# A transformer block with product-key experts: a shorter candidate list, fewer tiles ahead, and low parts summed by DMA

## The reference

```
q = (ht @ w_query).reshape(N, 8, 2, 128)
s1 = q[:, :, 0] . sub_keys_1 ; s2 = q[:, :, 1] . sub_keys_2      # 128 scores each
t1, i1 = top_k(s1, 16) ; t2, i2 = top_k(s2, 16)
cand = t1[..., :, None] + t2[..., None, :]                       # 256 pairs
sc, pos = top_k(cand.reshape(N, 8, 256), 16)
eidx = i1[pos // 16] * 128 + i2[pos % 16]
gate = softmax(sc)
out = sum over picks of gate * gelu(x . expert_down[eidx]) * expert_up[eidx]
```

## Time and profile before

| | |
|---|---|
| median of 3 runs | 1526.71 us (1525.58 to 1527.91) |
| profiled execution | 1529.9 us, span 1528.0 us |
| PE busy | 1503.2 us (98%) |
| DVE busy | 1226.5 us (80%) |
| ACT busy | 629.1 us (41%) |
| POOL busy | 534.3 us (35%) |
| PE clock granted | 0.997 |
| DMA | 378.94 MB, mean 248 GB/s |

### The profile page before, as it was taken

One profiled execution on the slowest core, in us unless ns is written; L12 is line 12 of the kernel. 1 busy time (PEld: TensorE's weight loads), 2 busy tenths in 40 slices (PEclk: granted clock), 3 DMA queues, 4 the chain that ended last, 5 costly groups with the idle time before them and its releaser, 6 DMA issues.

```text
span 1528.0 us, 22468 instructions
## 1 busy us (share of the span) xinstructions
PE 1503.2 (98%) x8379; PEld 1345.0 (88%) x8379; DVE 1226.5 (80%) x2329; ACT 629.1 (41%) x1050; POOL 534.3 (35%) x357
## 2 busy tenths in 40 slices
PE   9999999999999999999999999999999999999997
PEld 6888888889899999998888888999999999999996
DVE  5577885449999999975776776888888889888885
ACT  6247675332222356663333333333333333333335
POOL 0323102055755710002111112555555556555530
PEclk9999999999999999999999999999999999999999
DMA  8302003323323668889999989999999999999971
GB/s 313 146 25 87 1 2 128 117 89 112 131 60 114 173 208 307 320 307 368 299 309 301 302 293 339 363 367 370 356 361 370 362 371 361 369 367 356 371 254 69
DMA packets 148507, 378.94 MB, mean 248 GB/s; under 512 B 11792, under 2 KB 76688, under 8 KB 145456
## 3 DMA queue, kind: packets, MB, share of 16 engines
q1 hardware_dynamic: 100400, 201.84, 38.3%
q0 software_dynamic: 37200, 138.56, 24.5%
q10 hardware_dynamic: 10800, 37.11, 6.6%
HBM read 338.60 MB, written 38.86 MB: 247 GB/s over the span
## 4 chain that ended last, share of the span: by engine, by line
PE 85%; DVE 10%; DMA 2%; ACT 1%; issue 1%; SPq 0%; DVEq 0%; ACTq 0%
PE bank L1898 22%; PE bank L1803 20%; PE bank L1524 12%; PE bank L1904 11%; PE bank L1812 10%; PE bank L1735 2%; DVE oh L1406 2%; DVE gp L1414 2%; DVE gp L1411 2%; DVE oh L1409 2%; PE bank L1719 1%; DVE d_lo L1395 1%; DMA w_raw<-wts 1%; PE bank L1644 1%; PE bank L1821 1%
## 5 line engine op out<-in xcount | busy, mean ns | idle before, releaser
L1803 PE MATMUL bank<-h_hi,d_hi 128*128 128x384 f32 x1024 | 349.2, 341 | 1.1 <-DVE h_lo L1260 1.1
L1803 PE MATMUL bank<-h_lo,d_hi 128*128 128x384 f32 x1024 | 344.9, 337 | 0.0
L582 POOL DMA_INDIRECT p_in<-rows,p_row x128 | 160.5, 1254 | 403.7 <-DVE p_dot L1433 186.0
L582 POOL DMA_INDIRECT p_in<-up,p_row x128 | 172.0, 1344 | 191.5 <-DVE p_dot L1433 97.1
L1812 PE MATMUL bank<-h_hi,d_lo 128*128 128x384 f32 x1024 | 200.2, 338 | 0.0
L1803 PEld LDWEIGHTS bank<-h_hi,d_hi 128*128 128x128 f32 x1024 | 192.5, 188 | 4.0 <-issue 1.3
L1803 PEld LDWEIGHTS bank<-h_lo,d_hi 128*128 128x128 f32 x1024 | 192.4, 188 | 3.2
L1898 PE MATMUL bank<-u_hi,w_hi_e 128*128 128x512 f32 x750 | 192.2, 392 | 1.3 <-DVE w_lo_e L1458 1.3
L1898 PE MATMUL bank<-u_hi,w_lo_e 128*128 128x512 f32 x750 | 191.0, 390 | 0.0
L1904 PE MATMUL bank<-u_lo,w_hi_e 128*128 128x512 f32 x750 | 190.8, 390 | 0.0
L1812 PEld LDWEIGHTS bank<-h_hi,d_lo 128*128 128x128 f32 x1024 | 180.8, 188 | 0.0
(11 more groups left out here) (290 smaller groups left out, 2438.8 us busy)
## 6 DMA issues: line engine op xcount, KB each, us to landing
d_raw<-down SPq DMA_DIRECT2D x128, 512.0 KB, 5.7
u_raw<-up SPq DMA_DIRECT2D x128, 512.0 KB
gates_dram<-ev ACTq DMA_DIRECT2D x12, 2048.0 KB, 6.7
g_e<-gates_dram SPq DMA_DIRECT2D x32, 768.0 KB
w_raw<-wts SPq DMA_DIRECT2D x9, 2048.0 KB, 8.3
act_dram<-f_act ACTq DMA_DIRECT2D x59, 192.0 KB
a_e<-act_dram SPq DMA_DIRECT2D x59, 192.0 KB
xt<-x_in SPq DMA_DIRECT2D x2, 2048.0 KB, 11.1
```

The lines of the kernel that those rows point to most:

```text
L582: pool.indirect_dma_start(out=p_in[n % GR][:], out_offset=None, in_=rows if kind == "D" else up.rearrange("n p d -> (n p) d"), in_offset=b ...
L1803: nc.tensor.matmul(bank[6 + e % 2][:, 0:TD], d_hi[e % DH_R][:, k], h[:, k, 0:TD], start=(k == j == 0), stop=False)
```

## The change

- **Candidates.** With both lists sorted, pair (i, j) can be among the best 16 only where few pairs dominate it. Rows are cut by runs: row 0 keeps 16 columns, rows 1 and 2 keep 8, rows 3 to 6 keep 4, rows 7 to 14 keep 2, row 15 keeps 1: 65 pairs. They are added by five operations over all four token blocks, and the top 16 is sought among 65. All runs have 16 elements, but for the last, so the column is the position masked by 15 >> (position >> 4). The row is found by comparing the position with the start of each row (is_ge, a staircase in place of a one-hot), and the first key's indices are turned into differences so that the staircase sums to the index.
- **Tiles ahead.** E_SLOTS is 24 instead of 33. E_DVE is 26, E_GATES 28, NE 50. POOL_KEYS is moved to earlier tiles.
- **Low parts.** For tiles 3 to 20 (18 tiles) ACT writes −raw, rounded, to one of three d_sum tiles, and POOL issues a DMA that adds raw to it. POOL no longer subtracts there. PE waits for f_summed0 to 2.
- Several semaphores are merged; cstb_loaded becomes part of cst_loaded.

```diff
-E_SLOTS = 33
+E_SLOTS = 24
+ACC_FROM, ACC_TO = DH_R, E_SLOTS - 3
+def summed(f):
+    return ACC_FROM <= f < ACC_TO
+def sums(f):
+    return 16 * sum(g % 3 == f % 3 for g in range(ACC_FROM, f + 1))
-POOL_KEYS = {6: 0, 8: 1, 11: 2, 13: 3, 16: 4, 20: 5, 25: 6}
+POOL_KEYS = {6: 0, 8: 1, 10: 2, 12: 3, 15: 4, 17: 5, 21: 6}
+RUNS = [(0, 1, 16), (1, 2, 8), (3, 4, 4), (7, 8, 2), (15, 1, 1)]
...
-            sp.dma_start(cstb[:], consts_b[:, 0:6 * P]).then_inc(S("cstb_loaded"), 16)
+            sp.dma_start(cstb[:], consts_b[:, 0:6 * P]).then_inc(S("cst_loaded"), 16)
...
             def early_low(f):
+                if summed(f):
+                    pool.wait_ge(S("d_neg_done"), f - ACC_FROM + 1)
+                    pool.dma_start(d_sum[f % 3][:], d_raw[f % DR][:], accum_op=ALU.add)\
+                        .then_inc(S(f"f_summed{f % 3}"), 16)
+                    return
...
+                if summed(e):
+                    nc.scalar.activation(d_sum[e % 3][:], d_raw[e % DR][:], ACT.Copy, scale=-1.0).then_inc(S("d_neg_done"), 1)
                 nc.scalar.activation(d_hi[e % DH_R][:], d_raw[e % DR][:], ACT.Copy).then_inc(S("d_hi_done"), 1)
...
+            link(V.memset(fifteen[:], TOPK - 1))
...
-                for b in range(TB):
-                    V.tensor_tensor(cand[:, b], tv[r][0][:, b].unsqueeze(2).broadcast_to([P, TOPK, TOPK]),
-                                    tv[r][1][:, b].unsqueeze(1).broadcast_to([P, TOPK, TOPK]), ALU.add)\
-                     .then_inc(S("cand_done"), 1)
+                for q, (first, n, m) in enumerate(RUNS):
+                    at_q = ROW_STARTS[first]
+                    V.tensor_tensor(cand[:, :, at_q:at_q + n * m].rearrange("p b (i j) -> p b i j", j=m),
+                                    tv[r][0][:, :, first:first + n].unsqueeze(3).broadcast_to([P, TB, n, m]),
+                                    tv[r][1][:, :, 0:m].unsqueeze(2).broadcast_to([P, TB, n, m]), ALU.add)\
+                     .then_inc(S("pair_step"), 1)
...
-                V.tensor_copy(tif[r][0][:], ti[r][0][:])
+                V.tensor_scalar(quart[:], posn[:], 4, None, ALU.logical_shift_right).then_inc(S("pair_step"), 1)
+                V.tensor_copy(dif[r][:], ti[r][0][:]).then_inc(S("pair_step"), 1)
                 V.tensor_copy(tif[r][1][:], ti[r][1][:])
-                V.tensor_scalar(pab[r][0][:], posn[:], 4, None, ALU.logical_shift_right)
-                link(V.tensor_scalar(pab[r][1][:], posn[:], TOPK - 1, None, ALU.bitwise_and))
+                dve.wait_ge(S("pair_step"), 9 * hd + 6)
+                V.tensor_tensor(low_bits[:], fifteen[:], quart[:], ALU.logical_shift_right).then_inc(S("pair_step"), 1)
+                dve.wait_ge(S("pair_step"), 9 * hd + 7)
+                V.tensor_copy(tif[r][0][:, :, 0:1], dif[r][:, :, 0:1])
+                V.tensor_tensor(tif[r][0][:, :, 1:TOPK], dif[r][:, :, 1:TOPK], dif[r][:, :, 0:TOPK - 1], ALU.subtract)
+                dve.wait_ge(S("pair_step"), 9 * hd + 8)
+                V.tensor_tensor(pab[r][1][:], posn[:], low_bits[:], ALU.bitwise_and).then_inc(S("pair_step"), 1)
+                dve.wait_ge(S("pair_step"), 9 * hd + 9)
...
-                                    iota16.unsqueeze(1).broadcast_to([P, TB * TOPK, TOPK]), ALU.is_equal)\
+                                    (iota16 if s else starts).unsqueeze(1).broadcast_to([P, TB * TOPK, TOPK]),
+                                    ALU.is_equal if s else ALU.is_ge)\
...
-                if e < E_DVE:
-                    pe.wait_ge(S("f_lo_done"), e + 1)
+                if summed(e):
+                    pe.wait_ge(S(f"f_summed{e % 3}"), sums(e))
+                elif e < E_DVE:
+                    pe.wait_ge(S("f_lo_done"), pool_lows(e))
...
-                pe.wait_ge(S("gate_done"), 1)
+                pe.wait_ge(S("gate_step"), 2)
```

More of the change, by code:

```diff
@@ L65 @@
 PICKS = PH * TOPK
+RUNS = [(0, 1, 16), (1, 2, 8), (3, 4, 4), (7, 8, 2), (15, 1, 1)]
+PAIRS = sum(n * m for _, n, m in RUNS)
+ROW_STARTS = [sum(n * m for _, n, m in RUNS[:q]) + i * RUNS[q][2] for q in range(len(RUNS)) for i in range(RUNS[q][1])]
 def pick_order():
@@ L155, in build @@
     h_lo = sb("h_lo", [P, KC, T], F32R)
-    cst = sb("cst", [P, 432])
+    cst = sb("cst", [P, 448])
     ident = cst[:, 0:P]
@@ L161, in build @@
     iota16 = cst[:, 416:432]
+    starts = cst[:, 432:448]
     cstb = sb("cstb", [P, 6 * P], BF16)
@@ L258, in build @@
     at[0] = after_w
-    cand = sb("cand", [P, TB, TOPK, TOPK])
-    candw = sb("candw", [P, TB, TOPK * TOPK])
+    cand = sb("cand", [P, TB, 72])
+    candw = sb("candw", [P, TB, 72])
+    dif = [sb(f"dif{r}", [P, TB, TOPK]) for r in range(2)]
+    quart = sb("quart", [P, TB, TOPK], U32)
+    low_bits = sb("low_bits", [P, TB, TOPK], U32)
+    at[0] = after_w + 8192
     hit_0 = [sb(f"hit0{s}", [P, TB, TOPK, TOPK]) for s in range(2)]
@@ L274, in build @@
     g_sum = sb("g_sum", [P, TB, PH])
+    fifteen = sb("fifteen", [P, TB, TOPK], U32)
     slots = max(at[0], base + (TL + 8 * TG) * NK * 2 + 4 * D * 4 + 2 * NGB * TG * GB * 4)
@@ L294, in build @@
         d_raw.append(sb(f"d_raw{i}", [P, KC, P]))
+    d_sum = [place(f"d_sum{i}", [P, KC, P], F32R, (after_w + 4096, slots - 4128, slots)[i]) for i in range(3)]
     d_hi = [sb(f"d_hi{i}", [P, KC, P], F32R) for i in range(DH_R)]
@@ L642, in _ @@
             act.dma_start(posi[:], pos).then_inc(S("freq_loaded"), 16)
-            act.dma_start(cst[:, 384:432], consts[:, 384:432]).then_inc(S("freq_loaded"), 16)
+            act.dma_start(cst[:, 384:448], consts[:, 384:448]).then_inc(S("freq_loaded"), 16)
             act.wait_ge(S("pool_set"), 1)
@@ L853, in _ @@
                 if f == E_SLOTS - 1:
-                    act.wait_ge(S("score_shift"), 1)
+                    act.wait_ge(S("gate_step"), 1)
                     nc.scalar.activation(score[:], score[:], ACT.Exp).then_inc(S("score_exp"), 1)
@@ L1311, in top16 @@
             def top16(vals, idx, src, tmp):
+                first = top_count[0]
+                top_count[0] += 3 * TB
                 for b in range(TB):
[L1314 to L1315 removed]
+                    V.max(vals[b][:, 0:8], src[b]).then_inc(S("top_step"), 1)
                 for b in range(TB):
[L1317 removed]
+                    dve.wait_ge(S("top_step"), first + b + 1)
                     V.max_index(idx[b][:, 0:8], vals[b][:, 0:8], src[b])
[L1319 removed]
+                    V.match_replace(tmp[b], vals[b][:, 0:8], src[b], LOW).then_inc(S("top_step"), 1)
                 for b in range(TB):
[L1321 to L1322 removed]
+                    dve.wait_ge(S("top_step"), first + TB + b + 1)
+                    V.max(vals[b][:, 8:16], tmp[b]).then_inc(S("top_step"), 1)
                 for b in range(TB):
[L1324 removed]
+                    dve.wait_ge(S("top_step"), first + 2 * TB + b + 1)
                     last = V.max_index(idx[b][:, 8:16], vals[b][:, 8:16], tmp[b])
@@ L1348, in _ @@
+                dve.wait_ge(S("pair_step"), 9 * hd + 5)
                 link(top16([score[:, b, hd] for b in range(TB)], [posn[:, b] for b in range(TB)],
-                           [cand[:, b].rearrange("p i j -> p (i j)") for b in range(TB)],
-                           [candw[:, b] for b in range(TB)]))
-                V.tensor_copy(tif[r][0][:], ti[r][0][:])
+                           [cand[:, b, 0:PAIRS] for b in range(TB)],
+                           [candw[:, b, 0:PAIRS] for b in range(TB)]))
@@ L1368, in _ @@
             gv = g_sum[:].rearrange("p b h -> p (b h)").unsqueeze(2).broadcast_to([P, TB * PH, TOPK])
-            V.tensor_tensor(sv, sv, gv, ALU.subtract).then_inc(S("score_shift"), 1)
+            V.tensor_tensor(sv, sv, gv, ALU.subtract).then_inc(S("gate_step"), 1)
             last_keys()
@@ L1373, in _ @@
             link(V.reciprocal(g_sum[:], g_sum[:]))
-            V.tensor_tensor(sv, sv, gv, ALU.mult).then_inc(S("gate_done"), 1)
+            V.tensor_tensor(sv, sv, gv, ALU.mult).then_inc(S("gate_step"), 1)
             rows_of = lambda t: t[:, TDB].rearrange("p h k -> p (h k)")
             link(V.scalar_tensor_tensor(p_row[:], rows_of(key[0]), float(NK), rows_of(key[1]), ALU.mult, ALU.add))
-            dve.wait_ge(S("gate_done"), 1)
+            dve.wait_ge(S("gate_step"), 2)
             V.tensor_copy(p_gate[:], rows_of(score)).then_inc(S("rows_ready"), 1)
@@ L1811, in score_block @@
                 for k in range(KC):
-                    m = nc.tensor.matmul(bank[6 + e % 2][:, 0:TD], d_lo[e % DR][:, k], h_hi[:, k, 0:TD],
+                    low = d_sum[e % 3] if summed(e) else d_lo[e % DR]
+                    m = nc.tensor.matmul(bank[6 + e % 2][:, 0:TD], low[:, k], h_hi[:, k, 0:TD],
                                          start=False, stop=(k == KC - 1))
```

16 lines of the change are left out of this document (9 added, 7 removed).

## The result

The changed kernel takes **1530.75 us** (median of 9 runs, 1530.11 to 1533.59) against 1526.70 (9 runs of before): 1.003 times as long, 95% interval 1.0019 to 1.004. It is slower by 4.05 us, a little more than the 0.2% that can be told from no change. The profiled execution took 1533.6 us.

A forecast was written before the change was run, and what follows sets the result against it. The prediction took the kernel as PE-bound but for some 4 us in the one-hot stretch and a 1.3 us stall; +1.1 (tiles) + 1.4 (gates) + 0 = +2.5 us, on the median 1529.2 us, range 1523 to 1536.

The forecast's parts named there:

- Nine tiles moved: Nine down tiles leave the stretch before the slot transposes (37.45 us less) for the late rounds (38.52 more): net +1.1 us.
- the price of switching shapes: In late rounds, a down tile beside an up product takes 4.28 us, 0.12 more than alone, from switching matmul shapes.
- load: Faster rival: the late rounds' 0.12 us comes from DMA traffic; fewer picks might win back 8 us, 1520; chance 0.06.
- my part on constants: At the head of SP's queue: cstb counts on the same semaphore as cst, both loaded before the projections; cost 0.
- The end of DVE's work, undisturbed: Last head's gate product on DVE, without collisions, ends at 504.4 us, 2.4 ahead of PE reaching the transposes.
- DVE waits for key scores in every head: In the heads, DVE needs 19.3 us each, PE delivers key scores every 21.3, so DVE waits each time.
- The collisions: DVE's last head and closing beside GpSimd operations: exclusion costs 3.8 us, so gates end at 508.2.
- PE's wait, 1.4: At the slot transposes PE waits 1.4 us for the gate product; bounds 0 and 4.2.
- the first rival: Slower: PE stands at the transposes if the gate product ends after 508.8; worst wait 7.0 us, typical total 1531.5; chance 0.26.
- Sums by DMA, 0: Low parts of early tiles: sums land in an assumed 8 us, tile 20 allows 9.3, so PE never waits.
- The stall near 925: PE's 1.3 us stall where load_down restarts beside load_act: nothing taken off for it, bounds 0 to −1.3.

The follow-up runs named there:

- e3_layout: The kernel before with 64 more bytes reserved for the constants, so nearly all tiles behind them shift by 64 bytes, no instruction changed; 1520.60 us.
- e1_keys19: The changed kernel with GpSimd's two key products of head 6 put after tiles 19 and 20 instead of 21 and 22; 1521.32 us.

## Why the prediction was right, and where it was not

The time (1529.2 forecast, 1530.75 measured) and the sign were right, but by luck: two errors cancel in it. PE's wait and the slow clock behind it cost 8.1 us more than I had said (6.9 and 1.2), and the late rounds and the stall gave back 8.4 (7.1 and 1.3) that I had not counted. Two signs that I had named myself speak against the working: rounds were to take 8.36 us, and the wait for the gate product was to be 0 to 4 us. By its steps, on the profiled executions (span 1528.0 to 1531.8):

- **Nine tiles moved, +1.1.** The bound by PE and the place of the tiles were right: 76 rounds came. The price was not a constant. I took 0.12 us per round as the price of switching shapes, on the strength of 2.83 beside 2.77, and gave "load" 0.06 as the rival. Most of it was neither; a shift of tiles by 64 bytes made each of the 76 rounds 0.093 shorter, −7.1 us. The row that I read the price from does not follow the rounds: in the changed kernel the first down group after the one-hot products still takes 2.84, while those in the rounds take 2.78 (chain):

```profile
641.55 2.84 PE bank L1850 x16
```

  The kernel's text shows the shift (`cst` grows from 432 to 448 columns), and my part on constants looked only at semaphores.
- **The end of DVE's work, undisturbed: 504.4.** Measured 516.97, less 9.0 for the additions' collisions, 2.2 for the hit's and 1.3 by which this execution was late from tile 0 on (300.52, before 299.25; other executions differ as much, e3_layout had 297.22): 504.5. The terms were right one by one: top 16 3.49 (3.4 forecast), additions 0.71 in free heads, arithmetic 502.19 to 503.10 = 0.91 for 0.54 before (+0.3 forecast). What does not fit is "DVE waits for key scores in every head": it waited four times (26.3 us in all, for twice and 21.3 before), last at 464.8, which is where the chain leaves PE.
- **The collisions, 3.8: the step that failed.** They made 11.2. I scaled the cost of before by the share of time in which GpSimd works and let an operation collide once, by its kind: cand 2.2, the products 2.2, "4.2 if the hits collide as well". But a GpSimd operation that reads SBUF held up each DVE operation with two SBUF inputs that came while it ran, to its end, however short the DVE operation was. DVE operations with one input were not held up: the top 16 of 65 took 3.49 us beside the subtraction of 499.54, and 453.77 − 450.27 = 3.50 in a head with no GpSimd computation beside it. Four additions of 256 had taken 3.64 in the last head; five shorter ones took 9.68. How much of these 6 us comes from there being five and how much from the denser queue was not tested: no run has four additions in that queue, and with the queue thinned out five take 0.80 (e1_keys19). That more than one addition can be held up stood in the trace of before: head 1's four took 5.57 us from 361.84 on, with GpSimd operations at 361.54 and 363.89. The Trainium skill, "SBUF — State Buffer", section "Who interferes with whom", says "Issue order, not op shape, decides who blocks"; these rows agree. In the other direction, GpSimd's subtraction that was issued while DVE's first hit ran took 2.80 us for 2.39, and the second hit then waited for it:

```profile
503.78 2.80 POOL L576 TENSOR_TENSOR d_lo<-d_raw,d_hi 128x1024 fp32r<-128x1024 f32 x1 [1.85 <-ACT d_hi L831]
```

  The new POOL_KEYS, which put head 6's products among GpSimd's subtractions, made the queue dense just there: I counted seven operations in 26 us, but not that five of them stand without a gap where the additions come.
- **PE's wait, 1.4.** It was 8.3, and 1.2 more for the transposes at half clock, which I had not priced. PE was ready at 508.7 and not at 506.8, later by 1.3 for this execution's start and by 0.6 for slightly longer query rounds and tiles; the 508.8 that the first rival names as the point from which it decides stands in no sum of mine, which has 506.8. A wait of 8.3 us is that rival, whose worst case was 7.0 with a chance of 0.26.
- **Sums by DMA, 0.** Right: DMA issues, KB and us to landing,

```profile
d_sum<-d_raw POOLq DMA_DIRECT2D x18, 512.0 KB, 5.1
```

  5.1 us to landing in the median and 8.1 at most (8 assumed, 9.3 allowed), and PE waited for none. The further 2.5 us that I had feared for tile 20 did not show. Not foreseen were tiles alone at 4.24, 0.08 more for each of the tiles after 18.
- **The stall near 925, 0.** It went; PE's waits after have no such line. 1.3 us, the optimistic end.
- **Sum.** Up to the one-hots: −37.45 (tiles) + 1.3 (late start) + 0.6 (tiles at 4.24, query rounds slightly longer) + 8.3 + 1.2 = −26.0, as the chain has it. After them: 9 × 4.28 = 38.5, less 7.1 for the rounds, 1.3 for the stall and 0.3 unexplained: +29.8. Together +3.8.

## What to carry to other kernels

When DVE works beside GpSimd, count DVE's instructions with two SBUF inputs and not only their elements: each can wait for a whole GpSimd operation, so look at what GpSimd has queued at that time, and move its work to where DVE runs instructions with one input or is idle. When one engine is busy all the time, as PE is here, cheaper work on another gains nothing (the shorter list alone: 0.3 us), and making the fill-in work ahead of a hand-over shorter only turns that side work's end into a wait. And compare two kernels at equal addresses: a size changed in an early tile moved the time by 6 us here, and hid that much of the change's cost of 10.

## What was unexpected of the hardware

The pace of matmuls depended on where tiles lie in SBUF. Late rounds took 8.36 us without a shift, 8.37 at 128 bytes and 8.27 at 64; the same shift made projection products slower, 5.59 for 5.51 (at 128 bytes they stayed at 5.60, and query products fell from 5.59 to 5.49, so those are not a matter of 128 alone). And after a wait of 8.3 us PE, busy at clock 1.00 until then, worked at a granted clock of 0.50 from 517 to 521 us. GpSimd operations of 2.4 us stretched five DVE additions from 0.71 to 9.68 us, while DVE operations with one input beside them kept their time.
